# Feature weights applied while tokens are turned, a transform by even and odd tokens, banded pooling, and last-layer attention one head at a time

## The reference, cut to what matters

```python
mx = jnp.concatenate([latent_attention(q, k, v, kc, vc),               # 8 heads, 512 keys
      pool_mix(zx[..., KV_END:POOL_END], w_pool[i], pool_scale[i]),    # window means (2, 4, 8, 16) minus the token
      fourier_mix(zx[..., POOL_END:], w_four[i])], axis=-1)
x = x + ga1 * (mx @ w_out[i])
# fourier_mix: f = fft2(u, axes=(tokens 256, features 64)).real; y = f @ w_four
# pool_mix:    y = (mean over the window - u) @ w_pool, times pool_scale
```

## Time and profile before

| | |
|---|---|
| median of 3 runs | 1570.15 us (1569.11 to 1572.11) |
| the profiled execution: time, span of its trace | 1570.76 us, 1569.0 us |
| TensorE busy | 1386.0 us, 88% of the span |
| VectorE, ScalarE busy | 723.8 us, 489.2 us |
| loads | 395.02 MB, mean 252 GB/s |

### The profile page before, as it was taken

The page is one execution under the profiler, slowest core; times in us unless marked ns, Lnnn a source line. Parts: engine busy times, 40 slices in busy tenths (PEclk is TensorE's granted clock), DMA queues, the critical chain, the costliest instruction groups (busy, mean ns, idle before and its releaser), DMA issues.

```text
span 1569.0 us, 24703 instructions
## 1 busy us (share of the span) xinstructions
PE 1386.0 (88%) x10320; PEld 1044.5 (67%) x10320; DVE 723.8 (46%) x1353; ACT 489.2 (31%) x937; POOL 31.4 (2%) x29
## 2 busy tenths in 40 slices
PE   7999999999999999989999999999896667676564
PEld 4754577877778777847999999998653334333232
DVE  4556446555555564674655668676521011110101
ACT  3426423222122233454543444564410000000001
POOL 0000020000000001001000000000000000000000
PEclk9999999999999999999999999999998788878878
DMA  9728435745755572355356429245999999999996
GB/s 358 276 97 255 162 129 204 256 161 198 268 177 188 171 230 108 133 163 191 117 176 206 134 70 318 91 135 206 367 425 426 426 425 426 426 426 426 426 426 268
DMA packets 164459, 395.02 MB, mean 252 GB/s; under 512 B 11621, under 2 KB 124793, under 8 KB 134393
## 3 DMA queue, kind: packets, MB, share of 16 engines
q1 hardware_dynamic: 163624, 391.91, 66.7%
q10 hardware_dynamic: 720, 1.49, 0.2%
HBM read 392.32 MB, written 1.05 MB: 251 GB/s over the span
## 4 chain that ended last, share of the span: by engine, by line
PE 69%; DMA 23%; DVE 3%; ACT 2%; issue 1%; SPq 1%; DVEq 0%; ACTq 0%
DMA R<-in_w_dram 22%; PE ps L999 15%; PE ps L1005 15%; PE ps L1000 15%; PE ps L2862 3%; PE ps L1027 2%; PE ps L1021 2%; PE ps L1022 2%; PE ps L1302 1%; PE ps L629 1%; PE ps L1359 1%; PE ps L2912 1%; PE ps L1333 1%; PE ps L1609 1%; DMA R<-in_w_in_dram 1%
## 5 line engine op out<-in xcount | busy, mean ns | idle before, releaser
L968 DVE TENSOR_TENSOR WL<-R,WH 128x1024 fp32r<-128x1024 f32 (+1 forms) x202 | 225.2, 1129 | 129.5 <-ACT WH L958 129.4
L2862 PE MATMUL ps<-R,XG 128*32 128x256 f32 x2048 | 167.0, 484 | 119.6 <-DMA R<-in_w_dram 113.9
L999 PE MATMUL ps<-HH,WH 128*128 128x256 f32 (+2 forms) x872 | 272.5, 333 | 0.0
L1000 PE MATMUL ps<-HL,WH 128*128 128x256 f32 (+2 forms) x872 | 269.1, 331 | 0.0
L958 ACT ACTIVATE WH<-R 128x1024 fp32r<-128x1024 f32 (+1 forms) x202 | 191.1, 961 | 151.4 <-PE ps L1005 113.3
L2862 PEld LDWEIGHTS ps<-R,XG 128*32 128x32 f32 x2048 | 84.9, 133 | 195.7 <-issue 177.8
L999 PEld LDWEIGHTS ps<-HH,WH 128*128 128x128 f32 (+1 forms) x872 | 163.9, 188 | 24.5 <-issue 3.6
L1000 PEld LDWEIGHTS ps<-HL,WH 128*128 128x128 f32 (+1 forms) x872 | 163.2, 187 | 16.4
L1005 PE MATMUL ps<-HH,WL 128*128 128x256 f32 (+2 forms) x872 | 164.6, 331 | 0.0
L999 PE MATMUL ps<-GH,WH 128*128 128x512 f32 (+1 forms) x480 | 154.2, 340 | 0.0
L1000 PE MATMUL ps<-GL,WH 128*128 128x512 f32 (+1 forms) x480 | 153.5, 339 | 0.0
(11 more groups left out here) (484 smaller groups left out, 1716.1 us busy)
## 6 DMA issues: line engine op xcount, KB each, us to landing
R<-in_w_dram SPq DMA_DIRECT2D x192, 1024.0 KB, 26.4
R<-in_w_ada_dram SPq DMA_DIRECT2D x72, 1024.0 KB, 6.8
R<-in_w_gate_up_dram SPq DMA_DIRECT2D x40, 1024.0 KB, 7.8
R<-in_w_in_dram SPq DMA_DIRECT2D x20, 1024.0 KB, 10.6
R<-in_w_down_dram SPq DMA_DIRECT2D x16, 768.0 KB, 4.4
R<-in_w_down_dram SPq DMA_DIRECT2D x16, 640.0 KB, 4.2
R<-in_w_in_dram SPq DMA_DIRECT2D x8, 512.0 KB, 7.1
R<-in_w_out_dram SPq DMA_DIRECT2D x16, 256.0 KB, 4.4
```

Source lines behind the costliest of these rows:

```text
L968: last = e.tensor_tensor(L, w, H.bitcast(F32), ALU.subtract)
L999: e.matmul(b[0:n, 0:N], H[:, k, 0:n], xh(k, N), start=(k == 0), stop=False)
L1000: e.matmul(b[0:n, 0:N], H[:, k, 0:n], xl(k, N), start=False, stop=False)
L2862: mm = e.matmul(PS[4][32 * g:32 * g + 32, 0:256], x[:, 4 * hf + k, :], w[g // 2][:, k, 256 * (g % 2):256 * (g % 2) + 256], start=(hf == 0 ...
```

## The change

- Pooling weights and Fourier feature weights are applied before the token mix. For pooling, `pe_rows` multiplies by `WPF` where it transposed. For Fourier, `pe_feature_tables` makes cosine and sine tables of the features times `w_four` (`CSW`), and `pe_folded` applies them to the tile, for even and odd tokens apart. The mixer then needs one group of products per result: for pooling three pieces of a banded table (136, 16 and 120 columns), for Fourier four products of 128 columns, whose even and odd halves DVE adds and subtracts. `k_pool` is gone, its bands are in `k_mix`.
- ACT writes `GH` from the product's bank, and DVE makes `GL` from the same bank: the copy into `MU` is gone for attention and pooling.
- `pe_turn_queries` moves from the end of tile 8 into tile 9.
- Layer 1 attention goes by one head in three score banks (0, 1, 7), with the transposes three heads behind, and its four mixer groups stand between heads 2, 6, 10 and 17. `out` tile 0 takes its chunks in the order in which they get ready (`LAST_ORDER`).
- The 8 ada fills of layer 1 leave its attention: five go into the gap after layer 0's `down`, three into the gap after layer 1's `out`, in place of 5 and 4 empty products; their loads are planned there. The fill ahead of the sum goes behind it.

```diff
+    for w in range(4):
+        for x in range(2):
+            p = K_POOL + 272 * w + 136 * x
+            mix[:, p:p + 136] = pool[128 * x:128 * x + 128, w, 120 * x:120 * x + 136]
...
+        if i:
+            plan_ada(5)
         plan_queries(A["w_in"][i], 1, N)
-        consts.append((const_load("k_pool", 2048), const_load("k_mix", K_END)))
+        consts.append(const_load("k_mix", K_END))
         plan_tiles(A["w_in"][i], [768, 896], N)
         plan_tiles(A["w_in"][i], [1024, 1152], N)
-        plan_ada(8 if i else 16)
-        for load in consts[i]:
-            load.used = (s_mx, 30 if i else 20)
+        if i == 0:
+            plan_ada(16)
+        consts[i].used = (s_mx, 12 if i else 8)
-                if i == 0 and c == 0 and half == 0:
-                    plan_ada(8)
+                if c == 0 and half == 0:
+                    plan_ada(3 if i else 8)
...
+    LAST_ORDER = (4, 5, 0, 1, 6, 2, 7, 3)
...
+            if z == 0:
+                last = e.transpose(PS[7][:, 128 * a:128 * a + 128], ZT[z][:, 128 * a:128 * a + 128], ident)
+            else:
+                last = e.matmul(PS[7][:, 128 * a:128 * a + 128], ZT[z][:, 128 * a:128 * a + 128], WPF[:, z - 1, :], start=True,
+                                stop=True)
...
+    def pe_feature_tables(e, i):
+        kc = R[consts[i].slot]
+        e.wait_ge(d_ring[consts[i].slot], consts[i].landed)
+        e.wait_ge(d_wp, 128 * (i + 1))
+        e.wait_ge(s_z, 3 * i + 1)
+        for j in range(2):
+            for h, c in enumerate((K_CD, K_SD)):
+                last = e.matmul(PS[7][:, 256 * j + 128 * h:256 * j + 128 * h + 128], kc[:, c:c + 128], WPF[:, 2 + j, :], start=True,
+                                stop=True)
+        last.then_inc(s_ztr, 1)
+    def act_feature_tables(e, i):
+        e.wait_ge(s_ztr, 8 * i + 2)
+        e.activation(CSW[:, :, :], PS[7][:, :].rearrange("p (j n) -> p j n", j=2), ACT.Copy).then_inc(s_zf, 1)
...
+    def pe_folded(e, i, j, st):
+        e.wait_ge(s_evi, 10 * i + 8 + j + 1)
+        if j == 0 and st == 0:
+            e.wait_ge(s_z, 3 * i + 3)
+        else:
+            e.wait_ge(s_zf, folded_count(i, j, st) - 1)
+        for odd in range(2):
+            c = 256 * st + odd
+            last = e.matmul(PS[7][:, 256 * odd:256 * odd + 256], ZT[j][:, c:c + 255:2], CSW[:, j, :], start=True, stop=True)
+        last.then_inc(s_ztr, 1)
...
             pe_turn_keys(e, i)
+            pe_feature_tables(e, i)
         elif j == 8:
             pe_head_spread(e, i, 2)
+        elif j == 9:
+            for h in range(2):
+                pe_turn_queries(e, i, h)
+            pe_folded(e, i, 0, 0)
-            for h in range(2):
-                pe_turn_queries(e, i, h)
-        elif j == 9:
-            pe_rows(e, i, 8)
+        elif j == 9 and i == 0:
+            pe_folded(e, 0, 0, 1)
+    def act_in_end(e, i, j):
         if j == 9:
-            pe_rows(e, i, 9)
...
+    def act_value_out(e, A, m):
+        lo = 256 * A_STREAM[A]
+        e.wait_ge(s_pv, 8 * A + 2 * m + 2)
+        e.activation(GH[:, m, lo:lo + 256], values_bank(A, m)[:, 0:256], ACT.Copy).then_inc(s_gh, 1)
+    def dve_value_low(e, A, m):
+        lo = 256 * A_STREAM[A]
+        e.wait_ge(s_gh, out_index(A, m) + 1)
+        e.tensor_tensor(GL[:, m, lo:lo + 256], values_bank(A, m)[:, 0:256], GH[:, m, lo:lo + 256].bitcast(F32), ALU.subtract)\
+            .then_inc(s_gl, 1)
...
+    SCORE_BANKS = (0, 1, 7)
+    LAG = 3
+    MIX_AT = {2: 0, 6: 1, 10: 2, 17: 3}
+    def value_at(x):
+        return (x - 7) // 4 if 7 <= x < 20 and (x - 7) % 4 == 0 else None
+    def head_at(x):
+        return x // 4, x // 2 % 2, x % 2
...
+    def pe_last_attention(e):
+        for x in range(20):
+            if x < 16:
+                pe_last_scores(e, x)
+            if x == 1:
+                pe_folded(e, 1, 1, 0)
+            if x in MIX_AT:
+                pe_last_mixer(e, MIX_AT[x])
+            if value_at(x) is not None:
+                pe_values(e, 2, value_at(x))
+            if 3 <= x < 19:
+                pe_last_turn(e, x - LAG)
+    def act_last_attention(e):
+        for x in range(20):
+            if x < 16:
+                act_last_exp(e, x)
+            if x == 1:
+                act_folded(e, 1, 1, 0)
+            if 3 <= x < 19:
+                act_turned(e, 2, (x - LAG) // 2, (x - LAG) % 2)
+            if MIX_AT.get(x, 2) < 2:
+                act_pool_out(e, 1, MIX_AT[x], 0)
+            if value_at(x) is not None:
+                act_value_out(e, 2, value_at(x))
+            if MIX_AT.get(x, 0) >= 2:
+                act_four_odd(e, 1, MIX_AT[x] - 2, 0)
+            if MIX_AT.get(x - 1, 0) >= 2:
+                act_four_out(e, 1, MIX_AT[x - 1] - 2, 0)
+            if x == 13:
+                act_split(e, first_of["out", 1])
...
+    MIX = [(S, x) for x in range(4) for S in range(2)]
+    SPLIT_AT = 3
...
+    def pe_mixer(e, i, x, S):
+        kc, bank = R[consts[i].slot], mix_bank(i, x, S)
+        if x < 2:
+            for t, first, n, start, stop in ((0, 0, 136, True, False), (1, 120, 16, False, True), (1, 136, 120, True, True)):
+                for a in range(2):
+                    c = 128 + 128 * x + 64 * a
+                    p = K_POOL + 272 * (2 * x + a) + 136 * t + first - 120 * t
+                    last = e.matmul(bank[64 * a:64 * a + 64, first:first + n], Z[:, 2 * S + t, c:c + 64], kc[:, p:p + n],
+                                    start=start, stop=stop)
         else:
+            for odd in range(2):
+                for h in range(2):
+                    p = K_DFT + 256 * odd + 128 * h
+                    last = e.matmul(bank[:, 128 * odd:128 * odd + 128], ZF[x - 2][:, S, odd, 128 * h:128 * h + 128],
+                                    kc[:, p:p + 128], start=(h == 0), stop=(h == 1))
+        last.then_inc(s_mx, 1)
...
+    def act_pool_out(e, i, x, S):
+        lo = 256 * S
+        e.wait_ge(s_mx, mix_index(i, x, S) + 1)
+        e.activation(GH[:, 4 + x, lo:lo + 256], mix_bank(i, x, S)[:, 0:256], ACT.Copy, scale=pool_scale(i, x)).then_inc(s_gh, 1)
+    def dve_pool_low(e, i, x, S):
+        lo = 256 * S
+        e.wait_ge(s_gh, mix_out(i, x, S) + 1)
+        e.scalar_tensor_tensor(GL[:, 4 + x, lo:lo + 256], mix_bank(i, x, S)[:, 0:256], pool_scale(i, x),
+                               GH[:, 4 + x, lo:lo + 256].bitcast(F32), ALU.mult, ALU.subtract).then_inc(s_gl, 1)
...
+        e.activation(MU[sum_count(i, j, S) % 3][:, 256:384], mix_bank(i, j + 2, S)[:, 128:256], ACT.Copy).then_inc(s_zf, 1)
+        e.tensor_tensor(t[:, 0:128], even, t[:, 256:384], ALU.add)
+        e.tensor_tensor(t[:, 128:256], even, t[:, 256:384], ALU.subtract).then_inc(s_ot, 1)
...
-    BUSY = {2: 5, 3: 4, 4: 4}
+    BUSY = {4: 4}
...
-    GAP = {1: tuple(range(24, 32))}
+    GAP = {1: tuple(range(24, 32)), 2: tuple(range(32, 37)), 3: tuple(range(37, 40))}
-                fills = GAP.get(n, ()) if j == KT - 1 else ()
-                for a in fills[0:1]:
-                    pe_fill(e, a)
                 if j == KT - 1:
                     pe_sum(e, n, N)
-                for a in fills[1:]:
-                    pe_fill(e, a)
-                if j == KT - 1:
+                    for a in GAP.get(n, ()):
+                        pe_fill(e, a)
                     pe_busy(e, BUSY.get(n, 0))
```

More of the change, by code:

```diff
@@ L79, in constants @@
     mix = np.zeros((128, K_END))
[L80 to L85, removed]
+    for w in range(4):
[4 more added lines that the diff above has]
+        for h in range(2):
+            mix[:, K_DFT + 256 * odd + 128 * h:K_DFT + 256 * odd + 128 * h + 128] = dft[h, odd::2]
+    mix[:, K_R1:K_CD] = r1.T
     mix[:, K_CD:K_SD] = np.kron(np.eye(2), np.cos(ld) / 8.0)
@@ L995, in pe_tile @@
         e.wait_ge(*high[t])
-        for k in range(K):
+        order = LAST_ORDER if t == first_of["out", 1] else range(K)
+        for k in order:
             if ready is not None:
                 ready(k)
-            e.matmul(b[0:n, 0:N], H[:, k, 0:n], xh(k, N), start=(k == 0), stop=False)
+            e.matmul(b[0:n, 0:N], H[:, k, 0:n], xh(k, N), start=(k == order[0]), stop=False)
             e.matmul(b[0:n, 0:N], H[:, k, 0:n], xl(k, N), start=False, stop=False)
@@ L1365, in fills_at, with steps_of @@
     def fills_at(A, s):
-        return (8 * (1, 2, 4)[A] + s,)
-    def steps_of(group):
-        return [(A, s) for A in group for s in range(8)]
+        return (8 * (1, 2)[A] + s,)
+    def steps_of():
+        return [(A, s) for A in range(2) for s in range(8)]
     def pair_at(steps, x):
@@ new lines, in dve_last_max, with act_last_exp, pe_last_turn @@
+    def dve_last_max(e, x):
+        e.wait_ge(s_sco, 32 + x + 1)
+        e.tensor_reduce(stats(32 + x)[:, 0:1], PS[SCORE_BANKS[x % 3]][:, :], AX.X, ALU.max, negate=True).then_inc(s_max, 1)
+    def act_last_exp(e, x):
+        v = 32 + x
+        e.wait_ge(s_max, v + 1)
+        e.wait_ge(s_tn, v - 3)
```

(66 more changed lines are left out.)

306 lines of the change are left out of this document (153 added, 153 removed).

## The result

The changed kernel takes 1560.02 us (median of 5 runs, 1558.64 to 1564.28), against 1570.36 us of the kernel before, measured beside it (1569.11 to 1572.68). The ratio is 0.9937, with a 95% interval from 0.9926 to 0.9947: 10.3 us faster, and 8.0 us slower than the 1552.0 us of the forecast. It lies 1.5 us above 1558.5, the upper end of the range given for 8 in 10. The profiled execution took 1558.64 us, the lowest of the five.

The account below looks back on a forecast made before the run. Loads set the experts' end, but PE's slot releases hold their flow until near 1100 us. Terms 0.4 + 0.4 − 10.2 − 0.4 − 8.85 + 0.45 = −18.2 gave median 1552.0 us; own range 1549 to 1555, 8 in 10 1545 to 1558.5.

Parts of the forecast that it names:

- From there PE is packed: 14 lone scores at 1.06 = 14.8: Layer 1's attention from head 2 at +4.5: PE works without gaps, 14 single-head scores taking 14.8 us.
- the sum at full clock: Layer 1's attention with its mixers, first scores to `out`: PE's priced work and final steps reach +40.65 us.
- −8.85: Layer 1's attention and mixers together: 49.5 us before, 40.65 after, so 8.85 us saved.
- the chain of the heads: Layer 1's attention: each head's maximum-to-copy sequence stalls PE, 0.25 us a head, +3.5 us, 1555.5 us; chance 0.18.
- The lone score: Layer 1's attention: one head's score costs PE 1.06 us, as much as a pair; lower bound 0.53.
- the rival of the cheap score: Layer 1's attention: one head's score costs 0.53 us, DVE's 1.42 leads, 3.4 us less, 1548.6 us; chance 0.12.
- Layer 0's mixers: From the mixers' start to the first product of `out`: 19.45 us falls to 9.25, −10.2.
- the −11.5 of the bounds: Layer 0's mixer stage: the largest saving its price bounds allowed, in a range of −8.5 to −11.5 us.
- the mechanism of the forecast: End of layer 0's mixer stage: `out` waits for the bank of the third Fourier group's sum, 0.6 us, until 9.3.
- Fills in the gaps: Gaps after layer 0's `down` and layer 1's `out`: ada fills replacing empty products cost 0 each; first gap's bound +1 us.
- the rival of SP's queue: Layer 1's gate and up: loads queued behind `k_mix`'s late slot starve PE, +12 us net, 1582 us; chance 0.03.
- the rival of no change: Experts' loads: not held by PE's releases, so they start no earlier, 1570 us; chance 0.03.

Follow-up runs that it names:

- the second profile: The changed kernel run again with nothing changed and a profile of its own: 1562.63 us, ratio 0.9939 to the kernel before.

## Why the prediction was wrong

**The step that failed** is in layer 1's attention: "From there PE is packed: 14 lone scores at 1.06 = 14.8", with all products priced at full clock because the stages of before had it. The count, the order and the sum at full clock were right: 41.25 us at clock 1.00 against 40.65. But the new order put a wait of 2.46 us (the sum had 1.45 of it, since it priced the pair of heads 0 and 1 as two lone scores) ahead of a row of thin work, and took out the eight fills. The clock fell to half for 17.1 us (23.8 in the second profile), which cost 8.6, and −8.85 became −0.3 (+2.7). No rival had it: the chain of the heads, with 3.5 us, was the only stall considered, and it never came near: PE waited 4.5 us in the stretch in all, 2.46 ahead of head 2, 1.12 ahead of the third values, and 0.91 ahead of the last, where the sum had 1.0.

**Its cause** is shown as far as this: cover the wait and the 8 us come back (1551.97); leave 1.58 us of it and they don't (1560.37); put work in the attention and the clock holds (1557.08); issue pairs behind the same wait and it held in one profile and was back after 6.8 us in the other (by their times, four of the eight runs kept it); add dense products in the low clock and it is back. So a short wait can tip it, and thin work behind keeps it low. Which short wait tips it stays open: 1.12 us did in one profile of five, 1.86 us with pairs did not. What exactly the chip counts was not measured. The Trainium skill, "TensorE: Matmul & The Clock Gate", Part 1, says that the low clock is the default and that activity releases it. The run with eight products in the low clock agrees with the second half (back at 676.8, while they ran), and the changed kernel adds that PE busy in every microsecond (4.00 of 4.00 from 667 us, clock 0.50) need not be activity enough. The forecast had taken the clock of the old order for that of the stage.

**The lone score** costs what a pair does, 1.05 us to 1.06: right, as the earlier trace rows had it. So the rival of the cheap score is out. What follows from it was underrated: pairs were there to be had, and save 2.3 us at full clock.

**Layer 0's mixers** were right in kind, off by 1.4 us in size, just beyond the −11.5 of the bounds. The changed kernel's chain at their end, ACT and DVE, then PE:

```profile
166.76 1.83 PE L1733 MATMUL ps<-R,Z 128*64 128x136 f32 x36
...
167.53 1.58 ACT L1768 ACTIVATE GH<-ps,VEC 128x256 fp32r<-128x256 f32 x3
...
170.30 1.05 ACT L959 ACTIVATE WH<-R 128x1024 fp32r<-128x1024 f32 x1
...
172.94 1.22 DVE L969 TENSOR_TENSOR WL<-R,WH 128x1024 fp32r<-128x1024 f32 x1
...
174.28 0.28 DVE L1791 TENSOR_TENSOR MU<-ps,MU 128x128 f32<-128x128 f32 x1
...
174.62 0.50 PE L1003 MATMUL ps<-GH,WH 128*128 128x512 f32 x1 [0.97 <-DVE MU L1791]
```

Three pooling conversions took 1.58 us, 0.53 each, near the 0.57 taken. But ACT reached its split at 170.30, 3.5 us from the stage's start where the sum had 4.2, since a pooling group cost PE 0.59 (168.52 − 166.76 for three, the next product's start; 0.81 for six products was the nearest row, and by columns it was 0.57). DVE's additions of a group took 0.5 together and not 0.6, and ran while ACT copied. So DVE began its split 6.2 us from the start (172.94) where the sum had 7.5. PE's first product waited 0.97 us for the third group's sum (L1791), which is the mechanism of the forecast.

**The rest.** Fills in the gaps cost nothing (0.0 and −0.1), as argued; no PE wait in layer 1 was on a load, so the rival of SP's queue is out. What was saved ahead of the experts arrived at the end: −12.5 at 1041.5 (1029.05), −12.2 at the span's end, so the rival of no change is out too.

## What to carry to other kernels

Before thin work (few rows, small tiles, one head alone) is packed behind a wait, or fills are taken out of such a place, look at the granted clock as a cost of its own: every price read at full clock doubles if it falls. A few empty products inside a wait that is there anyway cost nothing and gave 8 us here. And where two products can share the array's rows, issue them together: the pair costs what one does, and in the one profile where the clock fell ahead of pairs it was back after 6.8 us. A single profile doesn't tell whether a wait is harmless: the same wait tipped the clock in one execution and not in another.

## What had not been expected of the hardware

- A wait of 1.58 to 2.46 us was enough to bring the clock to 0.50 when lone scores followed, in four profiles of four, but not with fills behind one of 1.46 us; with pairs behind it the clock held in one profile (2.45 us) and fell in another (2.46 us).
- The same wait of 1.12 us, with the same work around it, brought the clock to 0.50 for 3.4 us in one profile and left it at 1.00 in four.
- At the low clock PE was busy all the time for 17.1 us in one profile and for all but the first 0.3 of 23.8 us in the other, and the clock stayed low; in the run with eight dense products it came back while they ran.
- The empty products' operands are partly a matrix of ones; they held the clock like other work did.
